# Self attention in a three-block transformer program: normalise at the output instead of at the weights, and take norm squares on GpSimd

## What is computed

```python
def fox_attention(q, k, v, log_f):            # 8 heads of 64
    s = einsum(q, k) * scale + c_t - c_s      # c = cumsum(log f); s <= t
    p = softmax(s, axis=-1)
    return einsum(p, v)
def chunked_rel_attention(q, k, v, rel_bias): # 8 heads of 64
    s = einsum(q, k) * scale + bias           # a chunk and those left of it
    p = softmax(s, axis=-1)
    return einsum(p, v)
...
o_f = rms_norm(o_f.reshape(B, S, 512), g_fox_out)
o_c = rms_norm(o_c.reshape(B, S, 512), g_chunk_out)
mix = concatenate([o_f, o_c], -1) @ w_out
m = rms_norm(mem, g_mem_kv)                   # 256 rows; keys and values of the memory
```

## Time and profile before

| | us |
|---|---|
| runs, median (lowest to highest) | 2094.74 (2093.04 to 2095.23) |
| profiled execution, first to last instruction | 2090.6 |
| median of the runs less that span | 4.1 |
| self attention, first score product to the last weighing | 161.2 to 268.9 |
| TensorE, VectorE, ScalarE, GpSimd busy in the whole span | 2054.0, 1120.3, 875.4, 964.1 |

### The profile page before, as it was taken

How to read it: one execution, slowest core, us unless ns; L and a number is a source line. 1 busy time by engine, 2 the same in 40 slices (tenths; PEclk the granted TensorE clock), 3 DMA queues, 4 the chain that set the end, 5 groups by cost and what they waited for, 6 DMA issues and landing times.

```text
span 2090.6 us, 28050 instructions
## 1 busy us (share of the span) xinstructions
PE 2054.0 (98%) x9901; PEld 1688.7 (81%) x9901; DVE 1120.3 (54%) x1769; ACT 875.4 (42%) x1493; POOL 964.1 (46%) x489
## 2 busy tenths in 40 slices
PE   9999999999999999999999999999999999999997
PEld 7877787888888888787778888888777888888887
DVE  4525834335677776763385543434566635434345
ACT  5326864455222222534386322323476653232233
POOL 3437885453445545334235244444445752444443
PEclk9999999999999999999999999999999999999999
DMA  6530052214466664364323133332322031332332
GB/s 214 193 101 21 11 202 91 81 41 161 157 225 213 227 229 155 101 221 161 86 51 106 51 101 93 97 100 91 91 81 81 1 101 52 100 99 92 100 93 89
DMA packets 70325, 238.40 MB, mean 114 GB/s; under 512 B 7776, under 2 KB 11232, under 8 KB 70112
## 3 DMA queue, kind: packets, MB, share of 16 engines
q1 hardware_dynamic: 70240, 237.26, 35.4%
HBM read 231.20 MB, written 2.10 MB: 112 GB/s over the span
## 4 chain that ended last, share of the span: by engine, by line
PE 82%; DVE 6%; ACT 4%; POOL 4%; issue 3%; DMA 1%; DVEq 0%; SPq 0%; ACTq 0%; POOLq 0%
PE bank L942 25%; PE bank L944 25%; PE bank L943 25%; PE bank L1049 1%; PE bank L1176 1%; PE bank L1091 1%; POOL WL L806 1%; POOL sq L854 1%; PE bank L1064 1%; POOL t L854 1%; DVE bank L2508 1%; DVE acc L2394 1%; PE bank L1255 0%; POOL CW L879 0%; DVE x L2512 0%
## 5 line engine op out<-in xcount | busy, mean ns | idle before, releaser
L806 POOL TENSOR_TENSOR WL<-stage,WH 128x1024 fp32r<-128x1024 f32 x256 | 633.4, 2475 | 888.4 <-ACT WH L1675 883.1
L1675 ACT ACTIVATE WH<-stage 128x1024 fp32r<-128x1024 f32 x256 | 271.4, 1061 | 812.5 <-PE bank L944 799.9
L942 PE MATMUL bank<-H,WH 128*128 128x512 f32 (+1 forms) x1132 | 438.0, 387 | 2.6 <-DVE H L2418 2.1
L944 PE MATMUL bank<-H,WL 128*128 128x512 f32 (+1 forms) x1132 | 437.1, 386 | 0.0
L943 PE MATMUL bank<-H,WH 128*128 128x512 f32 (+1 forms) x1132 | 437.0, 386 | 0.0
L2757 DVE TENSOR_TENSOR Y<-bank,Y 128x512 f32<-128x512 f32 x328 | 215.6, 684 | 94.9 <-PE bank L944 94.2
L942 PE MATMUL bank<-HID,WH 128*128 128x512 f32 (+1 forms) x688 | 264.3, 384 | 0.1
L943 PE MATMUL bank<-HID,WH 128*128 128x512 f32 (+1 forms) x688 | 264.2, 384 | 0.0
L944 PE MATMUL bank<-HID,WL 128*128 128x512 f32 (+1 forms) x688 | 264.2, 384 | 0.0
L942 PEld LDWEIGHTS bank<-H,WH 128*128 128x128 f32 x1132 | 212.6, 188 | 47.9 <-issue 3.4
L944 PEld LDWEIGHTS bank<-H,WL 128*128 128x128 f32 x1132 | 212.6, 188 | 42.9
(11 more groups left out here) (468 smaller groups left out, 3612.2 us busy)
## 6 DMA issues: line engine op xcount, KB each, us to landing
stage<-panels SPq DMA_DIRECT2D x296, 512.0 KB, 3.6
ahead<-ada SPq DMA_DIRECT2D x102, 512.0 KB, 5.3
RAW<-panels SPq DMA_DIRECT2D x18, 512.0 KB, 4.0
apiece<-ada SPq DMA_DIRECT2D x10, 512.0 KB, 5.3
x<-xT SPq DMA_DIRECT2D x3, 1024.0 KB, 7.4
CS<-QKH SPq DMA_DIRECT2D x18, 128.0 KB, 2.4
outT<-x SPq DMA_DIRECT2D x16, 128.0 KB, 1.7
CS<-QKL SPq DMA_DIRECT2D x12, 128.0 KB, 2.4
```

Of the source, the lines that this page charges most:

```text
L806: pool.tensor_tensor(low_of(p, slot), stage[:, slot, :], high_of(p, slot).bitcast(F32), ALU.subtract).then_inc(s_split, 1)
L942: pe.matmul(out, wh, rh, start=start, stop=False)
L944: return pe.matmul(out, wl, rh, start=False, stop=stop)
L1675: act.activation(high_of(p, slot), stage[:, slot, :], ACT.Copy).then_inc(s_hisplit, 1)
```

## The change

Only the self attention changes. The weights stay unscaled exponentials (the maximum is still taken off). The values are held in VO with three slots of 64 columns: values of the even head, ones (zero in the low part), values of the odd head. A weighing takes two neighbouring slots, so that 64 rows of the bank hold the head's output and the other 64 its row sum, 64 times over. ScalarE takes Ln of the sums (`total_log`) and then exp of minus that (`inverse`) into `rstd`; VectorE multiplies the output rows by it while it writes them to Y (`out`). `invert`, `scale` and the accumulator's reads go for these heads. The squares of the memory, the fox and the chunk outputs go from ScalarE to GpSimd, and the adds 2 and 3 of the chunk outputs come after all outputs. The program's descriptor space is set to 1024 to make room for VO.

```diff
+        VO = place(156, "VO", [P, 2, 2, NT, 3, CH], F32R)
...
+                src = V[:, :, u // 4 * S + u % 4 * P:u // 4 * S + u % 4 * P + P]
+                return (src.rearrange("p a (h d) -> p a h d", d=CH), VO[:, u % 2, 0, :, 0:3:2, :], VO[:, u % 2, 1, :, 0:3:2, :])
...
+            def norm_square(name, m, source, width):
+                if m >= 2 or name != "mem":
+                    pool.wait_ge(s_add, first_of(ADD, name) + max(m - 1, 0))
+                pool.tensor_tensor(nsq[:, m % 2, 0:width], source, source, ALU.mult).then_inc(s_sq, 1)
+            def self_attention():
+                outs = att["self"]["out"]
+                low_v("self", 0)
+                low_v("self", 1)
+                for s in range(64):
+                    if s >= 12 and s % 8 == 7 and s // 8 + 1 < 8:
+                        low_v("self", s // 8 + 1)
+                    if 28 <= s < 36:
+                        if s == 28:
+                            pool.wait_ge(s_mem, 32)
+                        norm_square("mem", s - 28, memc(s - 28), MEM)
+                    if s in (36, 37, 39, 40):
+                        m = (36, 37, 39, 40).index(s)
+                        pool.wait_ge(outs, 2 * m + 2)
+                        norm_square("fox", m, Y[:, m, :], S)
+                    if s in (47, 55, 63):
+                        m = (s - 47) // 8
+                        pool.wait_ge(outs, 2 * m + 10)
+                        norm_square("chunk", m, Y[:, 4 + m, :], S)
+                pool.wait_ge(outs, 16)
+                norm_square("chunk", 3, Y[:, 7, :], S)
...
-                    pe.wait_ge(sm["probs"], s + 1)
+                    pe.wait_ge(sm["exp" if name == "self" else "probs"], s + 1)
...
+                        held = [VO[:, slot, hl, kb, n % 2:n % 2 + 2, :].rearrange("p h d -> p (h d)") for hl in range(2)]
...
-                        act.activation(Y[half_rows[n % 2], n // 2, :], O[n % 2][half_rows[n % 2], :], ACT.Copy)\
-                            .then_inc(sm["out"], 1)
+                def total_log(n):
+                    act.wait_ge(sm["pv"], weighed(name, n, 3))
+                    if n >= 2:
+                        act.wait_ge(sm["out"], n - 1)
+                    act.activation(rstd[half_rows[n % 2], :], O[n % 2][half_rows[1 - n % 2], :], ACT.Ln)\
+                        .then_inc(sm["total_log"], 1)
+                def inverse(n):
+                    act.wait_ge(sm["total_log"], n + 1)
+                    act.activation(rstd[half_rows[n % 2], :], rstd[half_rows[n % 2], :], ACT.Exp, scale=-1.0)\
+                        .then_inc(sm["inverse"], 1)
...
+                    if name == "self" and s >= 12 and s % 8 == 7:
+                        inverse(2 * (s // 8 - 1))
                     if s + 3 < steps:
                         exp(s + 3)
...
+                    if name == "self" and s >= 16 and s % 8 == 0:
+                        inverse(2 * (s // 8 - 2) + 1)
...
                         if s >= 12 and s % 8 in (6, 7):
-                            out(2 * (s // 8 - 1) + s % 2)
+                            total_log(2 * (s // 8 - 1) + s % 2)
...
+                def out(n):
+                    rows = half_rows[n % 2]
+                    dve.wait_ge(sm["inverse"], n + 1)
+                    dve.tensor_tensor(Y[rows, n // 2, :], O[n % 2][rows, :], rstd[rows, :], ALU.mult).then_inc(sm["out"], 1)
```

More of the change, by code:

```diff
@@ L597, in program @@
             att[name] = {k: sem(f"{name}_{k}") for k in (
-                "v_high", "v_split", "scores", "max", "exp", "recip", "probs", "turned",
-                "pt_high", "pt_split", "pv") + (("out",) if name == "self" else ())}
+                "v_high", "v_split", "scores", "max", "exp", "turned", "pt_high", "pt_split", "pv")
+                + (("total_log", "inverse", "out") if name == "self" else ("recip", "probs"))}
         s_pad = sem("queries_padded")
@@ L866, in attention @@
                         low_v(name, 1)
-                    if name == "self":
-                        if s >= 12 and s % 8 == 7 and s // 8 + 1 < 8:
-                            low_v(name, s // 8 + 1)
-                        continue
                     n = (s - 6) // 4
@@ L897, in _ @@
             split_lows(4, PANEL0["mem_k"])
-            attention("self")
+            self_attention()
             split_lows(PANEL0["mem_k"], RING0)
@@ L1243, in pv @@
                     high, low = weights_in(name, n)
-                    return three(O[n % 2][:, kb * P:S], VS[:, slot, 0, kb * P:(kb + 1) * P],
-                                 VS[:, slot, 1, kb * P:(kb + 1) * P], high[:, kb, kb * P:S], low[:, kb, kb * P:S],
+                    if name == "self":
+                        held = [VO[:, slot, hl, kb, n % 2:n % 2 + 2, :].rearrange("p h d -> p (h d)") for hl in range(2)]
+                    else:
+                        held = [VS[:, slot, hl, kb * P:(kb + 1) * P] for hl in range(2)]
+                    return three(O[n % 2][:, kb * P:S], held[0], held[1], high[:, kb, kb * P:S], low[:, kb, kb * P:S],
                                  kb == 0, kb == NT - 1)
@@ L1891, in self_norms @@
                     high_chunk("mem", s // 2 - 21, memc, lambda m: HMH[:, m, :], lambda m: col("zero"))
-                if s in (47, 55, 63):
-                    m = (s - 47) // 8
-                    act.wait_ge(att["self"]["out"], 2 * m + 10)
-                    norm_square("chunk", m, Y[:, 4 + m, :], S)
                 if s in (61, 63):
@@ L1914, in exp @@
                     act.wait_ge(sm["max"], s + 1)
+                    if name == "self":
+                        act.activation(prob[b][:, 0:w], score_bank(name, s)[:, 0:w], ACT.Exp, bias=stat[:, b:b + 1])\
+                            .then_inc(sm["exp"], 1)
+                        return
                     act.activation(prob[b][:, 0:w], score_bank(name, s)[:, 0:w], ACT.Exp, bias=stat[:, b:b + 1],
@@ L1972, in attention @@
                 if name == "self":
-                    out(heads - 2)
-                    out(heads - 1)
+                    inverse(heads - 3)
+                    total_log(heads - 2)
+                    inverse(heads - 2)
+                    total_log(heads - 1)
+                    inverse(heads - 1)
                     return
@@ L2118, in _ @@
             attention("self", self_norms)
-            act.wait_ge(att["self"]["out"], 16)
-            norm_square("chunk", 3, Y[:, 7, :], S)
             ring_panel(RING0 + 2)
@@ L2688, in out_low @@
                         .then_inc(s_h, 1)
-                maximum(0)
-                maximum(1)
-                invert(0)
-                maximum(2)
-                invert(1)
-                maximum(3)
-                invert(2)
+                def out(n):
+                    rows = half_rows[n % 2]
+                    dve.wait_ge(sm["inverse"], n + 1)
+                    dve.tensor_tensor(Y[rows, n // 2, :], O[n % 2][rows, :], rstd[rows, :], ALU.mult).then_inc(sm["out"], 1)
+                for s in range(4):
+                    maximum(s)
+                    if s and name != "self":
+                        invert(s - 1)
                 for s in range(steps):
@@ L2702, in attention @@
                         maximum(s + 4)
-                    if s + 3 < steps:
+                    if s + 3 < steps and name != "self":
                         invert(s + 3)
+                    if name == "self" and s >= 16 and s % 8 == 0:
+                        out(2 * (s // 8 - 2) + 1)
                     if late:
                         pt_low(s)
+                    if name == "self" and s >= 12 and s % 8 == 7:
+                        out(2 * (s // 8 - 1))
                     if name == "mem" and s >= 5 and s % 4 == 1:
@@ L2714, in attention @@
                         beside(s)
+                if name == "self":
+                    for n in range(heads_of(name) - 3, heads_of(name)):
+                        out(n)
+                    norm_add("chunk", 2, acc_chunk, S)
                 if name in WEIGHED:
@@ L2838, in _ @@
             dve.memset(onesr[:].bitcast(F32), 0.0).then_inc(s_eps, 1)
+            for slot in range(2):
+                dve.memset(VO[:, slot, 0, :, 1, :].bitcast(F32), 1.0)
+                dve.memset(VO[:, slot, 1, :, 1, :].bitcast(F32), 0.0)
             add_squares("x")
```

21 lines of the change are left out of this document (3 added, 18 removed).

## The result

The kernel after took **2120.76 us** (median of 4 runs, 2120.14 to 2121.49), the kernel before 2093.89 (2092.72 to 2095.23): ratio 1.0129, 95% interval 1.0115 to 1.0144, 26.9 us slower. The direction was forecast; the size was not: 2110, and 2119 at most.

The account below looks back on a forecast made before the run. TensorE, busy 98% of the program, was taken as the bound, so each new wait is lost in full. Interval changes from -1.2 before s = 6 to +7.5 at mem_k summed to +15.2: span about 2106, runs 2110 us, range 2100 to 2119.

Parts of the forecast that it names:

- the rival that did count falls: Self attention: the clock falls in every unit with a stand, six more falls, 2120 us; chance 0.1.
- three of those stands in its own sum: weigh(odd, 0) 2.0 us later at s = 31 and 3.4 at s = 39; TensorE stands 7.5 us ahead of mem_k.
- its own price of 1.7 a fall: TensorE's clock: a fall costs 3.4 us at half, 1.7 us lost.
- The tail: End of the attention: last weighings wait for out(12) and out(13), the latter behind ScalarE's second ring_panel; 6.81 to 8.4, +1.6 us.
- the start: Attention up to turn s = 6: TensorE's gaps put down to the scaling go, -1.2 us.
- What goes: Self attention: GpSimd's scalings, VectorE's reciprocals, ScalarE's accumulator reads go; -8.6 us if nothing takes their place.
- The outputs' chain: Weighings wait for Ln, exp, product: 1.1 us for the even head, 0.5 odd; 1.63 six times, 9.8 us.
- The squares: GpSimd, s = 31, 39: low_v ahead of squares, VectorE waiting; units 15.9 and 16.6 us, the 5.7 together bounded 1 to 9.
- The panel not yet split: Ahead of mem_k: GpSimd's squares 2 and 3 stand before the splits of panels 0 and 1; TensorE stands 7.5 us.
- that the outputs come in time: Rival: out(even) done before weigh(even, 0), TensorE waits in no unit, nor does the clock fall; 2092 us, chance 0.13.
- That half the chain waits: Rival on the outputs' chain: one of the two heads fits, 15.2 - 4.9, 2105 us; chance 0.17.
- That ScalarE becomes the bound: Rival: ScalarE's share stays but its order is worse, 3 us more, 2113 us; chance 0.1.

Follow-up runs that it names:

- the first of the filled kernels: Against the kernel after: 46 products without use added at the end of the attention and ahead of mem_k, no wait changed; 2119.88 us, ratio 1.0128.
- Filling the last two stands: Against the kernel with low_v behind the square at steps 31 and 39: 46 products without use added in TensorE's stands; 2106.92 us, ratio 1.0064.
- the experiment on the order alone: Against the kernel after: GpSimd's low_v goes behind the square at steps 31 and 39; 2111.8 us, ratio 1.0084.
- the kernel with the splits first: Against the kernel after: GpSimd splits the first two mem_k panels at step 63, ahead of the last two squares; 2115.84 us, ratio 1.0102.
- everything on GpSimd: Against after: early unscaled copy, GpSimd's products and squares, low_v behind squares, splits ahead of last squares; 2103.77 us, or 2103.51 with splits waiting for VectorE's sum.

## Why the prediction was wrong

The intervals of its sum, then what the profile after shows, with the low clock's share (half of the busy time at 0.50) taken apart:

```
interval           before  forecast  after  of it clock
to turn s = 6      173.81   172.6   174.42     -
s = 6 to 14         11.65    10.7    10.74     -
s = 14 to 22        11.81    12.7    13.09     -
s = 22 to 30        11.81    12.7    13.16     -
s = 30 to 38        13.99    15.9    18.04    1.7
s = 38 to 46        13.92    16.6    19.06    3.1
s = 46 to 54        12.52    13.3    13.43     -
s = 54 to 62        12.63    13.6    13.14     -
tail                 6.81     8.4    12.62    2.8
stand at mem_k       0        7.5     7.26     -
```

In mem_k itself the clock costs 2.8 us more by the count of halves, and 2.4 by the panels: from the first to the third it is 9.6 us here and 7.2 in the first of the filled kernels, at 1.00. The time of these panels was to be unchanged.

**The step that failed** is the clock. The sum counted no new fall ("The stand of 7.5 us may take over the fall of before, so it counts nothing by itself"), and the rival that did count falls tied them to every unit with a stand and had 0.1. Both were wrong. The four units with stands of 1.04 and 0.67 us alone keep the clock at 1.00 in this profile, so that the case which the page "TensorE: Matmul & The Clock Gate" of the Trainium skill tells of in its section "HAM oscillation — how this bites in real kernels", a fall in every round, does not show for waits as short as these. The clock is low in or right behind the stands of 2.46, 3.35, 4.17 and 7.21, once for 3.4 us, twice for 6.8 and once for 10.2, and stays low for part of the work that follows. The prediction had three of those stands in its own sum (2.0 and 3.4 us late, 7.5 long) and priced none of them; at its own price of 1.7 a fall they would have come to 5 us, since it took every fall to last 3.4 us. Half of 20.8 us against half of 3.35 makes 8.7. Filling the last two stands gave 3.5 to 4.9 us back, and shortening the first two gave back stand and fall together, 9 us.

With the clock the forecast would have been 2119, near the 2120.8 measured, but that would have been luck in part. The tail and the start, below, add 3.1 and 1.8 us, and against them stands another term of the sum. The runs were to lie 4.1 us above the profiled span; the profiled execution of after took 2121.05 for a span of 2119.3, only 1.8 more. The 4.1 came from setting one execution's span beside the median of others.

**The tail** was too small by 3.1 us even so (12.62 - 2.8 against 8.4 - 1.7, the fall it had before being in the 8.4). Its step named ScalarE's second ring_panel; in the trace the first one is late too. ScalarE's timeline after:

```profile
276.92 1.06 ACT L1715 ACTIVATE WX<-RAW 128x1024 fp32r<-128x1024 f32 x1 [1.29 <-DMA RAW<-panels]
277.88 0.58 ACT L1945 ACTIVATE PT<-bank 128x512 fp32r<-128x512 f32 x1
```

It stood 1.29 us for a load, then copied for 1.06, with the high copy of turn 62 queued behind it, and pt_low and out(12) behind that. Before, the same copy waited 0.39 us, at 262.06. The high copy starts 2.80 us behind its turn (275.08), before it was 1.16 (263.30 behind 262.14): 1.6 of the 3.1 us. This is read from the timeline; no run changes it alone, and the other 1.5 stay open.

**The start** was to gain 1.2 us; the attention began 0.8 later and took 0.2 less up to s = 6. The traces tell both. Ahead of turn 6 TensorE did not stand: the kernel has products without use there already, seven written between turns 5 and 6, and they take their time whether the weights come early or not. TensorE's timeline before, then after:

```profile
171.95 1.87 PE L1049 MATMUL bank<-onesr,identr 128*128 128x512 f32 x7
173.81 0.66 PE L1176 MATMUL bank<-con,sq 128*128 128x128 f32 x4
```

```profile
172.72 1.86 PE L1076 MATMUL bank<-onesr,identr 128*128 128x512 f32 x7
174.42 0.60 PE L1203 MATMUL bank<-con,sq 128*128 128x128 f32 x4
```

From the first of the seven to the turn it is 1.86 us before and 1.70 after, so 0.2 was all that could be had. The 0.8 arises in the first 13 us of the program, where ScalarE's squares of x wait for a load until 10.45 and not 9.61; in the kernel without division it is 9.80, and the attention begins at 161.34. Why the load lands later is open.

What was right. *What goes*: 10.74 for the unit without outputs (10.7), and the kernel without the division and with ScalarE's squares is 5 us faster than before, where the terms gave 8.6. Of the difference 1.0 is the start; in the attention before, the view of waits puts 4.4 us in 10 places down to the scaling and not 5.0 in 14; and VectorE's sum beside the splits, 2.87 us at 251.82, costs that kernel a stand of 1.8 us at 255.62. *The outputs' chain*: 1.04 and 0.67 us of wait for 1.1 and 0.5, in dense units; 13.1 for 12.7. *The squares*: order and place are right, low_v ahead of the square, VectorE behind it; without the clock the units take 16.3 and 16.0 for 15.9 and 16.6, and the experiment on the order alone confirms the cause. *The panel not yet split*: 7.21 us for 7.5, by the steps that were laid out. GpSimd's and VectorE's timelines after:

```profile
291.57 1.04 POOL L877 TENSOR_TENSOR nsq<-Y 128x512 f32<-128x512 f32 x1 [7.17 <-DVE acc_chunk L2639]
292.57 5.11 POOL L808 TENSOR_TENSOR WL<-stage,WH 128x1024 fp32r<-128x1024 f32 x2
```

```profile
290.74 0.69 DVE L2639 TENSOR_TENSOR acc_chunk<-acc_chunk,nsq 128x512 f32<-128x512 f32 x1
...
292.71 2.74 DVE L2639 TENSOR_TENSOR acc_chunk<-acc_chunk,nsq 128x512 f32<-128x512 f32 x1 [1.29 <-POOL nsq L877]
```

Sum 2, square 3, split, each behind the other; and sum 3 beside the split, 2.74 us.

*Of the rivals*: that the outputs come in time, 2092, is near what the kernel without the division does (2095.7, with three falls of the clock and 4.4 us ahead of mem_k). That half the chain waits did not come about. That ScalarE becomes the bound holds in part: 0.5 us in each dense unit goes with its work and not with the bank, though it is busy for no more than 19.9 of 23.6 us.

## What to carry to other kernels

Price a long stand of TensorE twice: its length, and the half-clock work behind it. In the kernel after, stands up to 1.1 us cost only their length, and those from 2.4 us on cost 1.7 to 3.1 more; but this is no limit, as the next section shows. Before moving small work to an idle engine, list what stands in that engine's queue on both sides of it and who waits for each: the squares took 1.04 us or less each, and cost 10 us through a split ahead of them and one behind them. And a normalization moved past a product should free the product's bank as early as the copy that it replaces: that took 1.4 us of the 2.2 in each dense unit away here, and even so no kernel with the division became faster than before.

## What the runs showed that was not expected

A clock fall is not tied to the length of one stand alone. In the kernel with the filled stands tried first, 1.64 us at the end of the attention had the fall of 278.2 behind it. In the kernel before, the fall of 262.1 lies at a stand of 0.71. And a pair of 1.05 and 0.68 us or nearly so had none in four units of the kernel after, but one in the kernel with the splits first (205.3). What decides is not taken apart by any run.

Contention is larger than the prediction counted: sums of 128x512 with both inputs in SBUF took 2.74, 2.82 and 2.87 us beside GpSimd's splits of 128x1024, about 0.7 without (0.68, 0.69); a maximum that reads a bank kept its 0.68 beside the same split (263.05, everything on GpSimd). So an early split on an idle GpSimd is not free.

GpSimd's square of 128x512 takes 1.04 us, where its subtraction and its product of two different tiles take about 1.3 (1.29 and 1.27).

Which kernel is 5 us better or worse did not always follow the profile: the two kernels with everything on GpSimd have medians 0.3 us apart with third panels 4.8 us apart (287.71 and 282.89); the profiled execution of the first took 2108.1, 4 us above its median. The runs of that kernel go with the clock: the two longest, 2108.1 and 2110.2, have a mean granted clock of 0.993, the four others, 2103.2 to 2103.9, have 0.996 or 0.997. So its profile shows one of the two executions with more time at the low clock, and the stand of 4.6 us in it need not be what its median has. What makes the clock differ between runs of one kernel was not tried.
